# The low half of every expert's second down piece moves from VectorE to GpSimd

## The chip, the cores and the metric

The kernel runs on one core of one Trainium2 chip. The metric is device time in microseconds, from runs of the whole program. Engines are called as in the profile: PE (TensorE), PEld (its weight loads), DVE (VectorE), ACT (ScalarE), POOL (GpSimd), SP (SyncE, which here only issues DMAs).

## What is computed

The reference is a transformer block with two attention mixers and a mixture of experts, followed by a second block of two layers (dilated attention, then a gated linear recurrence, each beside attention over a memory). All tensors are float32, the sequence has 512 tokens of 1024 columns. The change is in the mixture of experts:

```
for e in range(N_EXPERTS):                                  # 32 experts, 8 groups of 4
    hid = silu(h @ w_gate[e]) * (h @ w_up[e])               # 1024 -> 256
    out = out + (hid @ w_down[e]) * combine[:, e:e + 1]     # 256 -> 1024
```

Each token has one group (the argmax of the group logits) and in it two experts with weights; `combine` is zero elsewhere.

## The kernel before

**Products in three passes.** Every weight matrix is streamed from HBM in pieces of up to 128 x 1024 float32 (512 KB) and split into a high half (ACT, a copy that rounds to the type fp32r, line 948, `hi_done`) and a low half (the piece minus its high half, line 1572 on DVE, `lo_done`). Activations are split in the same way. PE multiplies hi*hi, hi*lo and lo*hi (`PASSES`).

**Buffers.** A piece lies in one of RAW = 6 raw slots (`wraw`), its halves in one of SPL = 4 slots each (`whi`, `wlo`). SP loads the pieces in order; a load into a raw slot waits for `lo_done` of the piece that was there six pieces earlier (line 703). ACT makes the high half of piece p + 4 when PE has used piece p (`piece_used`, line 947). DVE makes a low half when the high half is there, and PE waits for the low half (line 2759). Six pieces of the experts (`HELD`, the first down pieces of experts 1, 5, 9, ...) are loaded ahead into memory of their own.

**The expert stage.** Tokens of a group are gathered into 128 rows (an indirect DMA of GpSimd into `x_row`), transposed and split. Expert n takes four gate/up pieces, each for two blocks of rows of both matrices; then the down product of expert n - 1 follows with its two down pieces, 0 and 1. So the order of the pieces is gu n 0, 1, 2, 3, dn n-1 0, 1, and so on, six for each expert. Each piece is six 512-column matmuls on PE.

PE's order for expert n: gate_up pieces 0 and 1; `hidden_t(n - 1)`, two transposes of the previous expert's hidden values; for the last expert of a group `columns`, four transposes of the next group's gathered rows; gate_up pieces 2 and 3; for the last expert of a group `columns` again; then `down(n - 1)`.

DVE's order for expert n (line 2009 on) follows one instruction behind another: feed of gu 0 (which makes the low half of the piece four further on, dn n-1 0), `hidden_lo(n - 1)` (line 2016), feed of gu 1 (the low half of dn n-1 1), for the last expert of a group `gathered` (four operations, line 1918), feed of gu 2, `hidden(n)` (line 2011), feed of gu 3, `gathered` again, feed of dn 0, for the first expert of a group `expert_sums` of the group before (line 2024, two operations, `y_done`), feed of dn 1. ACT has the same order with its own halves (`hidden_hi`, `silu`).

**GpSimd in the stage.** It issues the gathers and scatters. For group g it waits until the group's sums are made (`y_done`), scatters the rows to `x_moe` (line 860), waits for that (`y_out`), and gathers group g + 2 into the same rows (line 849). After the last group it waits until the last down piece has landed, and reloads x1 from `x_moe` (line 867).

**Low halves on GpSimd.** `lo_by_pool(p)` names pieces that DVE's `feed` leaves out. Before the change these are the `BESIDE_PICKS`, 16 pieces of the gate projections in the stage of the sparse attention's index, made by a loop at line 823.

Of the kernel before, what the change touches and what calls it, by code (L numbers as in the profile page):

```python
# [36 lines left out]
NGRP, EPG, FF = 8, 4, 256  # L37
# [70 lines left out]
def build(nc, A, out):  # L108
    ctx = ExitStack()
    with ctx:  # L110
# [5 lines left out]
        def S(name):  # L116
            if name not in sems:
                sems[name] = ctx.enter_context(nc.semaphore(name))
            return sems[name]
# [120 lines left out]
        NEXP = NGRP * EPG  # L240
        EXPERT_ORDER = [what for n in range(NEXP + 1)
                        for what in ([("gu", n, q) for q in range(4)] if n < NEXP else []) + ([("dn", n - 1, b) for b in range(2)] if n else [])]
        piece_of = {what: P_MOE + j for j, what in enumerate(EXPERT_ORDER)}
# [47 lines left out]

        BESIDE_PICKS = range(chunks[CH["ga0"]]["first"] + SPL, chunks[CH["gb0"]]["first"] + chunks[CH["gb0"]]["count"] + SPL)

        def lo_by_pool(p):

            return p in BESIDE_PICKS

        def slot_cols(p):
            return pieces[p][1] * pieces[p][2]
# [7 lines left out]
        def raw_slot(p):  # L307

            if p in HELD:
                return held[HELD.index(p)][:, 0:slot_cols(p)]  # L310
            return wraw[:, ring_at(p) % RAW, 0:slot_cols(p)]

        def raw_loaded(p):

            if p in HELD:
                return raw_held[HELD.index(p)], 96
            return raw_in[ring_at(p) % RAW], 96 * (ring_at(p) // RAW + 1)
# [412 lines left out]
        def wait_tp_read(eng, name, n):  # L730

            for par in range(2):
                last = max(u for u in range(TPU[name], TPU[name] + n) if u % 2 == par) if n > 1 or TPU[name] % 2 == par else None
                if last is not None:
                    eng.wait_ge(tp_free[par], last // 2 + 1)
# [20 lines left out]
        def _(pool):  # L756
# [63 lines left out]
                    r = pool.tensor_scalar(wi_s, idx1[:, :, 320:328], H8 ** -0.5, None, ALU.mult)  # L820
                r.then_inc(S("b_rot"), 1)

            for p in BESIDE_PICKS:
                pool.wait_ge(hi_done, p + 1)
                pool.tensor_tensor(w_slot(wlo, p, p % SPL), raw_slot(p), w_slot(whi, p, p % SPL).bitcast(F32),
                                   ALU.subtract).then_inc(lo_done[p % SPL], 1)

            wait_tp_read(pool, "ob", 4)
            pool.dma_start(x1, A["x"][0].rearrange("(t p) d -> p t d", p=P)).then_inc(S("res1"), 16)
# [18 lines left out]
            def gather(g):  # L848
                pool.indirect_dma_start(x_row[g % 2], None, x_all, bass.IndirectOffsetOnAxis(slot_from[:, g:g + 1], 0)
                                        ).then_inc(S(f"x_row_in{g % 2}"), 16)  # L850
# [4 lines left out]
            gather(1)  # L855
            pool.wait_ge(S("x_moe_in"), 32)
            pool.wait_ge(S("slot_to"), 1)
            for g in range(NGRP - 1):
                pool.wait_ge(S("y_done"), 2 * g + 2)
                pool.indirect_dma_start(x_moe, bass.IndirectOffsetOnAxis(slot_to[:, g:g + 1], 0), x_row[g % 2], None  # L860
                                        ).then_inc(S(f"y_out{g % 2}"), 16)
                pool.wait_ge(S(f"y_out{g % 2}"), 16 * (g // 2 + 1))
                if g + 2 < NGRP:
                    gather(g + 2)
            pool.wait_ge(*raw_loaded(piece_of["dn", NEXP - 1, 1]))
            for t in range(NT):
                pool.dma_start(x1[:, t, :], x_moe[t * P:t * P + P, :]).then_inc(S(f"x_back{t}"), 16)
# [70 lines left out]
        def _(act):  # L938
# [538 lines left out]
            for hh in range(2):  # L1477
# [25 lines left out]
                def decay(n):  # L1503
                    act.wait_ge(S("gl_e"), n + 1)
                    if n % 9 == 6:
                        (d1, d2), (_, second) = halves(kq[n % 5], 64), halves(G64[:, n // 9 % 4, :], 64)
                        act.activation(d2, second, ACT.Exp)
                        act.activation(d1, d1, ACT.Exp).then_inc(S("gl_x"), 1)
                        return
                    act.activation(kq[n % 5], kq[n % 5], ACT.Exp).then_inc(S("gl_x"), 1)  # L1510
# [47 lines left out]
        def _(dve):  # L1558
# [8 lines left out]
            def feed(p):  # L1567

                if p >= NP or lo_by_pool(p):
                    return  # L1570
                dve.wait_ge(hi_done, p + 1)
                dve.tensor_tensor(w_slot(wlo, p, p % SPL), raw_slot(p), w_slot(whi, p, p % SPL).bitcast(F32),  # L1572
                                  ALU.subtract).then_inc(lo_done[p % SPL], 1)
# [564 lines left out]
            for hd in range(9):  # L2138
                for i in range(12):
                    step, r = attention_step(i)  # L2140
                    if hd:
                        u = dil_unit(hd - 1, r)
                        U = u["U"]
                        c = U % 4
                        nm, mx = att_nm[:, c:c + 1], att_mx[:, 3 * c:3 * c + 3]
                        if step == "scores":
                            dve.wait_ge(att_s, U + 1)
                            at = 0
                            for g, (src, _, keys, mask, scale) in enumerate(u["s"]):
                                w = keys.shape[1]  # L2150
                                ins = dve.tensor_tensor_reduce(d_s[:, at:at + w], src[:, 0:w], mask, scale, LOW,
                                                               ALU.add, ALU.max, mx[:, g:g + 1])
                                at += w
                            link(ins)
                            link(dve.tensor_reduce(nm, mx, AX.X, ALU.max))
                            dve.tensor_scalar(nm, nm, -1.0, None, ALU.mult).then_inc(att_m, 1)  # L2156
                        elif step == "probs" and (i != 4 or hd == 8):
                            dil_probs(hd, r)
# [224 lines left out]
        def _(pe):  # L2383
# [519 lines left out]
            for hd in range(9):  # L2903
                for i in range(12):
                    step, r = attention_step(i)
                    if hd:
                        u = dil_unit(hd - 1, r)
                        U, name = u["U"], f"da{r}_{hd - 1}"
                        if step == "scores":
                            if r == 0:  # L2910
                                wait_tp_read(pe, f"dk_{hd - 1}", 3)
                            if U > AU["dil"]:
                                pe.wait_ge(att_done, outs(U))
                            for dst, q, k, _, _ in u["s"]:
                                mm = pe.matmul(dst[:, 0:k.shape[1]], q, k, start=True, stop=True)  # L2915
                            mm.then_inc(att_s, 1)
                        elif step == "probs":
                            pe.wait_ge(att_p, U + 1)
                            transposes(name, 0, [d_s[:, P * b:P * b + P] for b in range(4)])
                            transposes(name, 1, [d_s[:, P * b:P * b + P] for b in (4, 5)])  # L2920
                        else:
                            if r == 0:
                                read_all(f"vd{hd - 1}")
                            wait_tp_read(pe, name, 2)
                            for b, v in enumerate(u["v"]):
                                mm = pe.matmul(D_OUT, d_pt[:, P * b:P * b + P], v, start=b == 0, stop=b == 5)  # L2926
                            mm.then_inc(att_o, 1)
# [135 lines left out]
```

## Time and profile before

| | us |
|---|---|
| median of 3 runs | 2029.57 |
| lowest and highest run | 2026.38, 2033.82 |
| the profiled execution | 2037.6 |
| its span, first to last instruction | 2035.9 |
| PE busy in the span | 1951.7 (96%) |
| DVE busy | 1170.0 (57%) |
| ACT busy | 1025.1 (50%) |
| POOL busy | 316.8 (16%) |

The matmuls of the gate and up pieces (line 2783) run from 518.8 to 806 us of the span. In the tables of the profile a group of instructions is one line of the kernel with one engine and operation; "busy" is the time in which at least one of them ran, and the idle time behind it is what the engine waited just before. PE's ends are modelled, and matmuls overlap: one of 512 columns shows 0.39 us, but the next starts 0.23 us after it. The granted clock of the whole span is 0.992 of full speed.

### The profile page before, as it was taken

Reading aid. Unit: us, or ns where it says so; the run is one execution under the profiler, and the core shown is the slowest. Engines: PE = TensorE matmul, PEld = TensorE weight load, DVE = VectorE, ACT = ScalarE, POOL = GpSimd, SP = SyncE. Lnnn points to the kernel's source line nnn. Section 1 sums busy time; section 2 is a strip of 40 time slices with the busy share of each in tenths; the row PEclk is TensorE's granted clock in tenths of the full one; section 3 lists DMA queues with packets and bytes.
Section 4 is the critical chain, followed back from the end, with each engine's and each line's share of the span. In section 5 each row is a group of like instructions: output and inputs, shape, how many; then the busy total and the mean of one; then the engine's idle time right before and its main releaser. Section 6 shows DMA issues by size and latency. Waiting matters only on the chain.

```text
span 2035.9 us, 27851 instructions
## 1 busy us (share of the span) xinstructions
PE 1951.7 (96%) x10487; PEld 1683.2 (83%) x10487; DVE 1170.0 (57%) x2306; ACT 1025.1 (50%) x1689; POOL 316.8 (16%) x419
## 2 busy tenths in 40 slices
PE   7999999999999998999999999999999999998998
PEld 7977878777787776789999999999788778887887
DVE  3345388554899998753454445444443546746762
ACT  4654544344787777653544454445342555344341
POOL 1601232010010101201211121112010001401310
PEclk9999999999999999999999999999999999999999
DMA  4411221145899999523222222223243512122121
GB/s 146 144 42 42 73 73 63 42 136 217 286 363 370 352 367 349 174 57 86 63 72 74 69 67 70 71 70 94 77 150 95 175 42 73 43 73 57 58 104 42
DMA packets 178017, 255.58 MB, mean 126 GB/s; under 512 B 13565, under 2 KB 92234, under 8 KB 177882
## 3 DMA queue, kind: packets, MB, share of 16 engines
q1 hardware_dynamic: 168832, 221.33, 33.7%
q0 software_dynamic: 8784, 31.92, 4.2%
q8 instruction: 85, 1.39, 0.3%
q10 hardware_dynamic: 266, 0.52, 0.1%
q14 instruction: 50, 0.41, 0.1%
HBM read 239.57 MB, written 14.16 MB: 125 GB/s over the span
## 4 chain that ended last, share of the span: by engine, by line
PE 69%; DVE 15%; DMA 6%; ACT 5%; issue 2%; POOL 1%; SPq 0%; ACTq 0%; DVEq 0%
PE pb L2412 49%; DVE wlo L1572 6%; PE pb L2440 5%; DMA wraw<-w_down 3%; PE pb L3000 2%; ACT whi L948 2%; PE pb L2926 2%; PE pb L2496 2%; PE pb L2509 2%; PE pb L2915 2%; DMA wraw<-w_up 1%; PE pb L2783 1%; DMA wraw<-w_mem_kv 1%; DVE arena L2178 1%; PE pb L3023 1%
## 5 line engine op out<-in xcount | busy, mean ns | idle before, releaser
L1572 DVE TENSOR_TENSOR wlo<-wraw,whi 128x1024 fp32r<-128x1024 f32 (+4 forms) x430 | 489.2, 1151 | 533.4 <-ACT whi L948 532.1
L2412 PE MATMUL pb<-whi,AT_hi 128*128 128x512 f32 (+4 forms) x1864 | 725.5, 389 | 13.2 <-DVE arena L2178 5.4
L2412 PE MATMUL pb<-whi,AT_lo 128*128 128x512 f32 (+4 forms) x1864 | 677.4, 363 | 0.0
L2412 PE MATMUL pb<-wlo,AT_hi 128*128 128x512 f32 (+4 forms) x1864 | 675.7, 362 | 0.0
L948 ACT ACTIVATE whi<-wraw 128x1024 fp32r<-128x1024 f32 (+4 forms) x446 | 440.4, 994 | 393.8 <-PE pb L2412 327.0
L2412 PEld LDWEIGHTS pb<-whi,AT_hi 128*128 128x128 f32 x1864 | 352.6, 189 | 58.8 <-issue 19.8
L2412 PEld LDWEIGHTS pb<-wlo,AT_hi 128*128 128x128 f32 x1864 | 353.0, 189 | 39.5 <-issue 6.5
L2412 PEld LDWEIGHTS pb<-whi,AT_lo 128*128 128x128 f32 x1864 | 351.7, 189 | 39.8
L2440 PE MATMUL pb<-arena 128*128 128x128 f32 (+1 forms) x1116 | 169.7, 279 | 28.8 <-ACT arena L984 5.7
L2440 PEld LDWEIGHTS pb<-arena 128*128 128x128 f32 (+1 forms) x1116 | 137.5, 146 | 63.5 <-issue 11.3
L2783 PE MATMUL pb<-whi,AT_hi 128*128 128x512 f32 x256 | 105.3, 411 | 3.2 <-DVE wlo L1572 1.6
L2783 PE MATMUL pb<-whi,AT_lo 128*128 128x512 f32 x256 | 101.2, 395 | 0.0
L2783 PE MATMUL pb<-wlo,AT_hi 128*128 128x512 f32 x256 | 100.9, 394 | 0.0
L928 POOL TENSOR_TENSOR arena<-arena 128x256 f32<-128x256 f32 x72 | 64.3, 898 | 210.4 <-ACT arena L1510 200.8
L771 POOL TENSOR_TENSOR arena<-arena 128x64 f32<-128x64 f32 (+3 forms) x41 | 18.2, 444 | 479.6 <-DVE small L2193 333.3
L3000 PEld LDWEIGHTS pb<-arena 128*128 128x128 f32 x576 | 74.5, 191 | 9.6 <-issue 2.4
L3000 PE MATMUL pb<-arena 128*128 128x64 f32 (+2 forms) x576 | 76.0, 276 | 3.7 <-POOL arena L928 2.5
L1510 ACT ACTIVATE arena<-arena 128x512 f32<-128x512 f32 x64 | 39.5, 630 | 70.3 <-DVE arena L2295 54.6
L984 ACT ACTIVATE arena<-pb 128x512 f32<-128x512 f32 (+2 forms) x89 | 47.7, 571 | 37.4 <-PE pb L2440 37.4
L1040 ACT ACTIVATE arena<-pb,small 128x64 f32<-128x64 f32 x64 | 20.2, 316 | 87.2 <-PE pb L2509 87.2
L2783 PEld LDWEIGHTS pb<-whi,AT_hi 128*128 128x128 f32 x256 | 48.8, 191 | 17.9 <-DVE wlo L1572 7.5
L1401 ACT ACTIVATE arena<-arena,small 128x768 f32<-128x768 f32 x32 | 30.1, 940 | 63.5 <-DVE small L2156 63.5
(321 smaller groups left out, 2602.6 us busy)
## 6 DMA issues: line engine op xcount, KB each, us to landing
wraw<-w_in_a SPq DMA_DIRECT2D x288, 128.0 KB
wraw<-w_gate SPq DMA_DIRECT2D x128, 256.0 KB
wraw<-w_up SPq DMA_DIRECT2D x128, 256.0 KB
wraw<-w_down SPq DMA_DIRECT2D x58, 512.0 KB
wraw<-w_in_b SPq DMA_DIRECT2D x40, 512.0 KB
wraw<-w_in SPq DMA_DIRECT2D x28, 512.0 KB
wraw<-w_mem_kv SPq DMA_DIRECT2D x16, 512.0 KB
wraw<-w_in_a SPq DMA_DIRECT2D x16, 512.0 KB
```

Source lines behind the costliest of these rows:

```text
L928: pool.tensor_tensor(e2, q2, e2, ALU.mult).then_inc(S("gl_q"), 1)
L948: act.activation(w_slot(whi, p, p % SPL), raw_slot(p), ACT.Copy).then_inc(hi_done, 1)
L984: act.activation(dst, src, ACT.Copy, scale=scale).then_inc(tp_free[u % 2], 1)
L1572: dve.tensor_tensor(w_slot(wlo, p, p % SPL), raw_slot(p), w_slot(whi, p, p % SPL).bitcast(F32), ALU.subtract).then_inc(lo_done[p % SPL], 1)
L2412: mm = pe.matmul(ACC[bank][:, 0:n], a, b, start=kc == 0 and q == 0, stop=i == c["count"] - 1 and kk == per - 1 and q == 2)
L2440: tr = pe.transpose(TP[u % 2][0:b.shape[1], at:at + P], b, ident)
L2496: pe.matmul(SC[U % 2][:, 0:u["kw"]], u["q"], u["k"], start=True, stop=True).then_inc(att_s, 1)
L2509: mm = pe.matmul(TP[tu % 2][:, 0:u["dv"]], pt[:, P * b:P * b + P], u["v"][b], start=b == 0, stop=b == nb - 1)
L2783: mm = pe.matmul(ACC[n % 2].rearrange("p (w f) -> p w f", w=2), a, b, start=k == 0 and m == 0, stop=k == 7 and m == 2)
L2915: mm = pe.matmul(dst[:, 0:k.shape[1]], q, k, start=True, stop=True)
L2926: mm = pe.matmul(D_OUT, d_pt[:, P * b:P * b + P], v, start=b == 0, stop=b == 5)
L3000: mm = pe.matmul(dst, tile(k, s), rhs, start=True, stop=True)
```

## The change

GpSimd makes the low half of piece `("dn", n, 1)` for all 32 experts, and DVE leaves these pieces out. The helper `low_half` is the body of the old loop. The 32 calls are put into GpSimd's list between its waits, scatters and gathers: three before the loop over groups, four in each of its seven rounds, and one behind it. Nothing else is changed: the pieces, slots, semaphores and the orders of SP, ACT and PE are the same.

```
+        EXPERT_PICKS = [piece_of["dn", n, 1] for n in range(NEXP)]
+
         def lo_by_pool(p):
-            return p in BESIDE_PICKS
+            return p in BESIDE_PICKS or p in EXPERT_PICKS
...
+            def low_half(p):
                 pool.wait_ge(hi_done, p + 1)
                 pool.tensor_tensor(w_slot(wlo, p, p % SPL), raw_slot(p), w_slot(whi, p, p % SPL).bitcast(F32),
                                    ALU.subtract).then_inc(lo_done[p % SPL], 1)
+            for p in BESIDE_PICKS:
+                low_half(p)
...
             pool.wait_ge(S("slot_to"), 1)
+            for p in EXPERT_PICKS[0:3]:
+                low_half(p)
             for g in range(NGRP - 1):
+                low_half(EXPERT_PICKS[EPG * g + 3])
                 pool.wait_ge(S("y_done"), 2 * g + 2)
                 pool.indirect_dma_start(x_moe, ..., x_row[g % 2], None).then_inc(S(f"y_out{g % 2}"), 16)
+                low_half(EXPERT_PICKS[EPG * g + 4])
                 pool.wait_ge(S(f"y_out{g % 2}"), 16 * (g // 2 + 1))
                 if g + 2 < NGRP:
                     gather(g + 2)
+                low_half(EXPERT_PICKS[EPG * g + 5])
+                low_half(EXPERT_PICKS[EPG * g + 6])
+            low_half(EXPERT_PICKS[NEXP - 1])
             pool.wait_ge(*raw_loaded(piece_of["dn", NEXP - 1, 1]))
```

## Rows read from the trace of the kernel before

**Rows 1.** The page's 40 slices: DMA, busy share in tenths.

```profile
DMA  4411221145899999523222222223243512122121
```

**Rows 2.** Stretches: us, then engines' busy time (instructions), PE clock, DMA share, GB/s.

```profile
598.00:634.00 36.00, 35.13 (x162) 28.52 (x161) 33.80 (x43) 28.90 (x40) 3.85 (x2) 1.00 1.00 364
...
sum 254.12, PE 248.38 PEld 198.97 DVE 236.40 ACT 205.97 POOL 20.25; mean PE 35.48 PEld 28.42 DVE 33.77 ACT 29.42 POOL 2.89
```

**Rows 3.** Instructions of one line: ns min/median/max, first and last start in us.

```profile
L2011 DVE SCALAR_TENSOR_TENSOR arena<-pb,arena x32: 472/478/484, 528.7 to 807.9; 128x256 f32<-128x256 f32 x32
```

**Rows 4.** Waits of PE from 526 to 800 us: total, times, longest.

```profile
PE pb L2806 <- DVE AT_lo L2016: 2.2, 4, 1.1
PE pb L2783 <- DVE wlo L1572: 1.6, 6, 0.4
PE pb L2806 <- DVE wlo L1572: 1.5, 2, 0.8
PE pb L2440 <- DMA arena<-x_all,arena: 1.4, 2, 0.9
```

**Rows 5.** The instructions of GpSimd's line 825.

```profile
L825 POOL TENSOR_TENSOR wlo<-wraw,whi x16: 2357/2392/2413, 238.5 to 355.9; 128x1024 fp32r<-128x1024 f32 x16
```

**Rows 6.** Timeline of DVE, 590 to 603 us: start, duration, instruction.

```profile
590.09 3.48 DVE L1572 TENSOR_TENSOR wlo<-wraw,whi 128x1024 fp32r<-128x1024 f32 x3
...
598.76 1.28 DVE L2024 TENSOR_TENSOR arena<-pb,arena 128x512 f32<-128x512 f32 x2
...
602.23 0.41 DVE L2016 TENSOR_TENSOR AT_lo<-pb,AT_hi 128x256 fp32r<-128x256 f32 x1
602.56 2.35 DVE L1572 TENSOR_TENSOR wlo<-wraw,whi 128x1024 fp32r<-128x1024 f32 x2
```

**Rows 7.** Timeline of the stage of the index, 252 to 256 us.

```profile
252.50 0.62 DVE L1835 SCALAR_TENSOR_TENSOR arena<-arena,small 128x384 f32<-128x384 f32 x1 [0.73 <-DVE arena L1820]
...
253.44 2.39 POOL L825 TENSOR_TENSOR wlo<-wraw,whi 128x1024 fp32r<-128x1024 f32 x1 [5.42 <-ACT whi L948]
...
254.54 1.70 DVE L1835 SCALAR_TENSOR_TENSOR arena<-arena,small 128x384 f32<-128x384 f32 x1 [0.56 <-DVE arena L1820]
```

**Rows 8.** Timeline of the recurrence, 1731 to 1734 us.

```profile
1731.50 1.21 DVE L1572 TENSOR_TENSOR wlo<-wraw,whi 128x1024 fp32r<-128x1024 f32 x1
1732.04 1.38 POOL L928 TENSOR_TENSOR arena<-arena 128x256 f32<-128x256 f32 x1 [1.09 <-ACT arena L1510]
1732.63 1.07 DVE L2293 TENSOR_TENSOR arena<-arena 128x256 f32<-128x256 f32 x1
```

**Rows 9.** Timelines of GpSimd and DVE behind the expert stage.

```profile
847.89 2.86 POOL L890 TENSOR_SCALAR arena<-arena,small 128x1024 f32<-128x1024 f32 x1
...
848.12 0.75 DVE L1595 SCALAR_TENSOR_TENSOR AT_lo<-pb,arena,AT_hi 128x512 fp32r<-128x512 f32 x1 [2.23 <-ACT AT_hi L978]
```

**Rows 10.** Timeline of PE: first matmuls of D1, gate/up piece 3, D1.

```profile
595.62 0.39 PE L2806 MATMUL pb<-whi,AT_hi 128*128 128x512 f32 x1
...
601.30 0.42 PE L2783 MATMUL pb<-whi,AT_hi 128*128 128x512 f32 x1
...
604.21 0.39 PE L2806 MATMUL pb<-whi,AT_hi 128*128 128x512 f32 x1
```

**Rows 11.** GpSimd's scatters: one of the timeline, and all of line 860.

```profile
600.32 2.85 POOL L860 DMA_INDIRECT x_moe<-arena  x1 [26.24 <-DVE arena L2024]
...
L860 POOL DMA_INDIRECT x_moe<-arena x7: 1178/2852/2855, 564.9 to 784.7; - x7
```

**Rows 12.** Timeline of ACT: the high half of D1.

```profile
591.85 1.05 ACT L948 ACTIVATE whi<-wraw 128x1024 fp32r<-128x1024 f32 x1
```

**Rows 13.** The stage's end: PE's last down product; the reloads of x1.

```profile
813.22 0.47 PE L2806 MATMUL pb<-whi,AT_hi 128*128 128x512 f32 x1 [3.77 <-DVE AT_lo L2016]
...
L867 POOL DMA_DIRECT2D arena<-x_moe x4: 548/562/577, 807.3 to 809.0; - x4
...
DMA to landing us min/median/max: 7.3/9.4/12.0
```

More of the change, by code:

```diff
@@ L821, in _ @@
                 r.then_inc(S("b_rot"), 1)
-            for p in BESIDE_PICKS:
+            def low_half(p):
                 pool.wait_ge(hi_done, p + 1)
```

## The prediction

> **What bounds the kernel now.** The page's 40 slices come first: the change touches only the expert stage, and the row of DMA shares shows that stage as the block of nines in the tenth to sixteenth slices [rows 1]. The reader is to see that three quarters of the kernel have nothing to do with this change. Then the stage is cut into stretches of about 36 us, which is one group of four experts (31 experts pass from 528.7 to 807.9, 9.0 us each [rows 3]). In the stretch from 598 us PE is busy for 35.1 us, DVE for 33.8, and the DMA engines have a share of 1.00 at 364 GB/s [rows 2]. Three resources run side by side within a few per cent. Over seven stretches PE is busy for 248.4 of 254.1 us [rows 2], and its waits with a named releaser are short: 2.2 us for the low half of the hidden activations (L2016), 1.6 and 1.5 us for weight low halves (L1572), 1.4 us for a gather [rows 4]. PE is the bound; DVE, which makes all low halves, sets how much lead PE's operands have. So the question is not what the 32 subtractions cost DVE, but whether the lead survives when one in six goes to a slower engine.
>
> **The price of one piece.** GpSimd does this very operation in an earlier stage: 2.39 us for 128x1024, sixteen times, 2.36 to 2.41 us [rows 5]. DVE runs three of them in 3.48 us, one every 1.13 us when they are queued (the last one's end adds 0.09) [rows 6]. So 32 x 1.13 = 36 us leave DVE, and 32 x 2.39 = 76 us come to GpSimd, which is nearly idle in the stage. Were the engines independent, GpSimd's piece would only be ready 1.3 us later than DVE's.
>
> They are not independent. While GpSimd ran L825 from 253.44 to 255.83, a DVE operation with two SBUF inputs (L1835) took 1.70 us and ended 0.41 us after GpSimd; the same shape took 0.62 us just before [rows 7]. The other way round, GpSimd's operation at 1732.04 was held until DVE's low half ended at 1732.71 and ended 0.71 us after that, and DVE's next two-input operation ended 0.28 us after GpSimd's [rows 8]. So such operations exclude each other for their whole length, and GpSimd gets in between two of DVE's. An operation that reads PSUM and one SBUF tensor is not held: L1595, begun beside a GpSimd instruction, took 0.75 us [rows 9]; the hidden and gathered low halves are of that kind.
>
> The Trainium skill has this as a rule (SBUF — State Buffer, section "SBUF: two separate sides"): VectorE and GpSimd share one port pair as an exclusive lock, not as a split of bandwidth, and a DVE operation with two SBUF inputs contends for it with a GpSimd operation that reads SBUF. The rule speaks against this change; by it the piece costs DVE's list more than it frees, without it the lateness below would be about half. The trace agrees with it, by the 1.70 us against 0.62.
>
> For one group of four experts the time that DVE's list needs goes from 33.8 us [rows 2] by 4 x (2.39 - 1.13) = +5.0 to 38.8 us, beyond the 36.0 of the period [rows 3]. What can run beside GpSimd comes off: four hidden_lo at 0.33 us [rows 6] and one of the two runs of gathered, four PSUM-fed operations of half hidden_lo's columns, which I put at 1.1 us by that row. That leaves 36.4 to 38.8 us.
>
> **Walk through one group.** GpSimd's four pieces are laid into the times at hand. D1 is an expert's second down piece, and "late" is against PE's present start of it.
> - First (D1 before the gathered halves): DVE runs these beside GpSimd, and PE has its own transposes of the gathered rows before D1. Cost 0.
> - Second: DVE's three low halves run to 593.57 [rows 6], so GpSimd has 593.5 to 595.9; PE wants D1 at 595.62 [rows 10]. Late by 0.3 us. DVE resumes at 595.9 with low half, hidden (0.4), two low halves, the sums (L2024, 1.20) and one more low half: 595.9 + 4 x 1.13 + 0.4 + 1.2 = 602.0. PE wants that last one at 601.30 + 0.3 = 601.6 [rows 10]. Late by another 0.4 to 0.5. Together 0.8.
> - Third: the scatter (L860) is issued 0.3 us after the sums and occupies GpSimd for 2.85 us [rows 11], now from 601.2 to 604.05, since the sums end 0.9 later. Behind it in GpSimd's queue stands low_half: 604.1 to 606.5, against 604.21 + 0.8 = 605.0 [rows 10]. Late by 1.5 us, 2.3 in all. DVE's next low halves, held until 606.5, are then just in time.
> - Fourth: ACT makes the high half of D1 only after PE has used the piece four before and after hidden_hi: about 0.9 us, then 1.05 [rows 12], 2.39, and 0.2 for three hand-overs: 4.6 us. PE gets to D1 in three pieces of 1.4 us (601.30 to 604.21 is two [rows 10]) and 0.3 us of transposes: 4.5 us. Late by 0.1.
>
> That is 2.4 us per group, for the seven groups with sums and a scatter: 16.8 us. Two of the seven scatters are short (minimum 1.18 us, median 2.85 [rows 11]); there the third item is about 0.9 less: -1.8. PE's waits for a gather, 1.4 us [rows 4], are swallowed by the delay: -1.4. The first group has three D1 at 0.1 to 0.2: +0.5. Sum +14.1 us.
>
> **What else moves.** SP loads into a raw slot when its low half is made, and in order; a D1 slot is freed up to 2.8 us later (606.5 against 602.56 + 1.13 = 603.7 [rows 6]), and all later loads queue behind. PE is delayed too, by up to 2.3 of that; I take 0 and keep up to 1 us per group for the range. At the end of the stage the reloads of x1 (L867) went out at 807.3, when the last down piece had landed; now high half and low half stand before them, 1.05 + 2.39 = 3.5 us. They land 7.3 to 12.0 us after issue, so at 818.1 to 822.8; their reader comes after PE has ended the last down product, 813.22 + 4.5, and a first matmul behind it, 818 at the earliest [rows 13]. Between 0 and 4.8 us; I take 0, since the first tile is wanted first and was issued first. The waits on y_done and y_out (L859 to L864 of the kernel before) hold nothing that PE wants sooner: the low half in front of y_done is of an expert whose product the sums need anyway, and the next gather waits some 7 us more for the scatter to land, longer than the low half before it takes.
>
> Bounds of the whole: below, -5.3 us, if all of PE's waits for DVE in the stage vanish; above, 8 x 5.0 = +40 us, if nothing overlaps and PE feels all of it.
>
> **Rivals.**
> - *Hidden.* DVE idles for 36.0 - 33.8 = 2.2 us per group, and the delays are absorbed there: the loads catch up in them, and DMA, at 364 GB/s and a share of 1.00 [rows 2], goes on setting the period. Price: the low end of DVE's list, 36.4 against 36.0 us, 8 x 0.4 = +3.2 us. For it: the share of 1.00. Against it: PE has no idle time from which to give a delay back. The Trainium skill has a rule that points this way (same page, section "A bandwidth-pool intuition that's wrong"): HBM gives a core about 358 GB/s, by which the loads are at their ceiling. The trace has 364 in the stretch, so at or near it.
> - *Faster.* GpSimd's 2.39 us fall into DVE's idle time and beside its PSUM-fed operations, so DVE's list is shorter by 1.13 us where PE waits for it: PE's 5.3 us of waits for DVE [rows 4] go, and so do the 3.77 us that PE waits for L2016 at the end of the stage [rows 13]: -9.1 us. It decides only where D1 has at least 1.3 us of lead; at 604.21 DVE's low half had ended at 603.7, a lead of 0.5.
> - *Full price.* The high half of D1 is ready just when a two-input operation is next in DVE's list, nothing overlaps, and PE runs dry each time: +40 us. For it: two of the four steps above have a margin of 0.1 to 0.3 us. Against it: hidden_lo and gathered stand exactly at D1's place in DVE's list.
>
> **How the numbers follow.** The profiled execution took 2037.6 us (span 2035.9 and 1.7 around it); the median of the runs, 2029.6, is 8.0 lower, and I carry the difference over. Forecast +14.1: 2051.7 for a profiled execution, 2043.7 for the median; chance 0.52, its own range +6 to +24. Hidden: 2032.8, chance 0.25. Faster: 2020.5, chance 0.09. Full price: 2069.6, chance 0.14. About 0.5%, 10.1 us, is what a measurement can tell from no change. Of the forecast's 0.52, 0.44 lies above +10.1. So slower 0.44 + 0.14 = 0.58, same 0.08 + 0.25 = 0.33, faster 0.09. For 8 in 10 the range holds the forecast and Hidden, a third of Faster and half of Full price: 2025 to 2064.
>
> **What would show it.** GpSimd's group of low halves grows from 16 to 48 with a mean near 2.4 us or a little above; DVE's L1572 group has 32 fewer, and some that follow GpSimd take over 2 us instead of 1.22; PE waits at L2806 for GpSimd in most experts, longest (over 1 us) behind a scatter; a group takes 38 to 39 us; the DMA share falls to about 0.95. I would be wrong if groups still take 36 us (Hidden), if no DVE low half takes longer than 1.3 us (no exclusion), if PE's new waits are for gathers or loads (the slot release and the queue, which I took as 0), or if time moves outside 510 to 830 us.

## The result, and the profile after

The kernel after takes 2038.57 us (median of 15 runs, 2033.90 to 2042.37), the kernel before 2033.10 in the same comparison (15 runs, 2026.26 to 2039.22): a ratio of 1.0031, interval 1.0020 to 1.0041, so about 6.3 us slower (4.1 to 8.3). That is clear of the noise, inside the 0.5% that the prediction called no change, inside its range, and well short of the forecast's +14.1 us. The profiled execution after took 2038.1 us, the one shown before 2037.6: the second was 4.5 above its own median, the first at its own, so the two profiles differ by less than the runs do. What they can show is where the time within the stage is, not its sum.

The page first: DMA and GpSimd in 40 slices, and then, for the stretch of [rows 2], the same columns as there (us, busy time and instructions of each engine, PE clock, DMA share, GB/s), with the sum over the seven stretches.

```profile
POOL 1601232010233334201211121112010001401310
...
DMA  4511222146899999423222222223243512122131
```

```profile
598.00:634.00 36.00, 35.43 (x160) 27.68 (x159) 33.32 (x39) 28.66 (x40) 12.71 (x6) 1.00 0.99 359
...
sum 254.12, PE 247.82 PEld 195.64 DVE 234.29 ACT 204.67 POOL 86.80; mean PE 35.40 PEld 27.95 DVE 33.47 ACT 29.24 POOL 12.40
```

GpSimd's busy time in the seven stretches rises from 20.25 us [rows 2] to 86.80. DVE lost 28 operations of 1.2 us in them, some 34 us, and its busy time fell by only 2.1 (236.40 to 234.29): the rest is mostly time in which its other low halves were held. PE's busy time fell by 0.6 us. The DMA share of the stretch shown is 0.99 (1.00 before), where I had said 0.95.

The instructions of three lines: ns min/median/max, first and last start. GpSimd's low halves are 48 with a median of 2.40 us; DVE's longest low half is now 3.09 us (1.88 before); and the scatters, which occupied GpSimd for a median of 2.85 us [rows 11], take 1.72, all seven.

```profile
L1584 DVE TENSOR_TENSOR wlo<-wraw,whi x398: 547/1212/3087, 14.2 to 2010.6; 128x1024 fp32r<-128x1024 f32 x140, 128x768 fp32r<-128x768 f32 x48, 128x672 fp32r<-128x672 f32 x4, 128x384 fp32r<-128x384 f32 x3
...
L827 POOL TENSOR_TENSOR wlo<-wraw,whi x48: 2357/2402/3147, 238.6 to 807.6; 128x1024 fp32r<-128x1024 f32 x48
...
L868 POOL DMA_INDIRECT x_moe<-arena x7: 1712/1718/1721, 563.5 to 784.1; - x7
```

The waits of PE from 526 to 800 us (total, times, longest), against [rows 4]: those for a DVE low half fell from 3.1 us to 0.2, those for a gather (1.4) are gone, and the new one is for GpSimd, 3.4 us in ten waits. The four waits for L2016 (2.2 us) have become one of 2.6 us; what it is comes with the end of the stage, below. PE's weight loads wait for GpSimd too, so these rows are no full account.

```profile
PE pb L2818 <- POOL wlo L827: 3.4, 10, 0.9
PE pb L2818 <- DVE AT_lo L2028: 2.6, 1, 2.6
PE pb L2795 <- DVE wlo L1584: 0.2, 1, 0.2
```

One group in the timelines (start, duration, instruction, idle time before it and its releaser): GpSimd, then DVE, then three first matmuls of PE. It is the group that the prediction walked through, and PE is 1.3 us earlier in this profile.

```profile
591.87 2.40 POOL L827 TENSOR_TENSOR wlo<-wraw,whi 128x1024 fp32r<-128x1024 f32 x1 [7.15 <-ACT whi L960]
599.51 1.71 POOL L868 DMA_INDIRECT x_moe<-arena  x1 [5.23 <-DVE arena L2036]
601.25 2.50 POOL L827 TENSOR_TENSOR wlo<-wraw,whi 128x1024 fp32r<-128x1024 f32 x1
607.05 1.29 POOL L854 DMA_INDIRECT arena<-x_all,arena  x1 [3.30 <-DMA x_moe<-arena]
610.50 2.41 POOL L827 TENSOR_TENSOR wlo<-wraw,whi 128x1024 fp32r<-128x1024 f32 x1 [2.17 <-ACT whi L960]
```

```profile
588.30 3.48 DVE L1584 TENSOR_TENSOR wlo<-wraw,whi 128x1024 fp32r<-128x1024 f32 x3
591.70 0.41 DVE L2028 TENSOR_TENSOR AT_lo<-pb,AT_hi 128x256 fp32r<-128x256 f32 x1
593.16 2.20 DVE L1584 TENSOR_TENSOR wlo<-wraw,whi 128x1024 fp32r<-128x1024 f32 x1 [1.04 <-ACT whi L960]
...
601.75 3.08 DVE L1584 TENSOR_TENSOR wlo<-wraw,whi 128x1024 fp32r<-128x1024 f32 x1
```

```profile
594.33 0.50 PE L2818 MATMUL pb<-whi,AT_hi 128*128 128x512 f32 x1
...
600.41 0.50 PE L2795 MATMUL pb<-whi,AT_hi 128*128 128x512 f32 x1
...
603.80 0.50 PE L2818 MATMUL pb<-whi,AT_hi 128*128 128x512 f32 x1 [0.27 <-POOL wlo L827]
```

The exclusion is as forecast. GpSimd's piece of 591.87 ends at 594.27 and PE starts on it at 594.33; the DVE low half that stood ready from 593.16 took 2.20 us and ended 1.1 us after GpSimd. Behind the scatter GpSimd ran from 601.25 to 603.75, PE started at 603.80, and DVE's low half was held for 3.08 us. What is not as forecast is the size: from D1's first matmul at 594.33 to the next D1 at 603.80 are 9.47 us, against 8.59 [rows 10]. I had said 2.3 us late in all, 0.3 of it already at the first of the two, so 2.0 more between them; it is 0.9.

The matmuls of one line are too uniform for a view to group them by step, so I took each piece's first matmul from PE's timeline and the mean distance from one piece's start to the next, over groups 1 to 7 (the gather's row and the last one over groups 1 to 6). Groups and experts are counted from 0. D0 and D1 are the down pieces, gu0 to gu3 the gate/up pieces; the distance is named by the piece that it leads to. Here and below, a piece's e is the place in PE's order: D0 and D1 of e=1 stand behind the gate/up pieces of e=1 and belong to the expert before. The prediction's first step is then D1 of e=3, the second D1 of e=0 and gu3 of e=1, the third D1 of e=1, the fourth D1 of e=2. The two last columns are experiments (E6, E7 below). The steps left out differ by 0.12 us or less between before and after, and by 0.05 or less between E6 and E7.

```
us to the start of       before  after    E6     E7
D0 of e=0                 1.46   1.76    1.44   1.39
D1 of e=0                 1.38   1.43    1.37   1.43
gu0 of e=1 to 3 (mean)    1.37   1.47    1.37   1.46
gu3 of e=1 (past sums)    1.46   1.68    1.46   1.72
D0 of e=1                 1.57   1.49    1.38   1.52
D1 of e=1 (past scatter)  1.44   1.81    1.38   1.88
D0 of e=2                 1.70   1.39    1.36   1.36
gu2 of e=3 (gather)       2.34   1.97    1.99   1.98
four experts             36.35  36.40   34.64  35.88
```

### The profile page after: what moved, and what is told of

Its sections match the earlier page's. It is cut to its first block, busy times and chain, and to the rows that moved or that the text cites. A ratio compares the mean times of both kernels' runs of the same rounds, so it can differ in the third digit from the quotient of the medians.

```text
span 2036.5 us, 27851 instructions
## 1 busy us (share of the span) xinstructions
PE 1953.6 (96%) x10487; PEld 1682.8 (83%) x10487; DVE 1168.0 (57%) x2274; ACT 1026.4 (50%) x1689; POOL 391.9 (19%) x451
## 4 chain that ended last, share of the span: by engine, by line
PE 74%; DVE 12%; ACT 6%; DMA 4%; issue 3%; POOL 2%; SPq 0%; ACTq 0%; DVEq 0%; POOLq 0%
PE pb L2424 49%; PE pb L2452 5%; PE pb L2795 4%; DVE wlo L1584 4%; ACT whi L960 2%; PE pb L3012 2%; PE pb L2938 2%; PE pb L2818 2%; PE pb L2508 2%; PE pb L2521 2%; PE pb L2927 2%; DMA wraw<-w_up 1%; DMA wraw<-w_down 1%; DVE arena L2190 1%; DMA wraw<-w_mem_kv 1%
## 5 line engine op out<-in xcount | busy, mean ns | idle before, releaser
L1584 DVE TENSOR_TENSOR wlo<-wraw,whi 128x1024 fp32r<-128x1024 f32 (+4 forms) x398 | 482.6, 1226 | 530.8 <-ACT whi L960 529.8
L2424 PEld LDWEIGHTS pb<-whi,AT_hi 128*128 128x128 f32 x1864 | 352.6, 189 | 58.6 <-issue 19.8
L827 POOL TENSOR_TENSOR wlo<-wraw,whi 128x1024 fp32r<-128x1024 f32 x48 | 116.9, 2436 | 252.4 <-ACT whi L960 252.3
L2795 PE MATMUL pb<-whi,AT_hi 128*128 128x512 f32 x256 | 104.3, 408 | 1.5 <-DVE AT_lo L1930 0.7
L2818 PE MATMUL pb<-whi,AT_hi 128*128 128x512 f32 x128 | 54.8, 428 | 10.4 <-DVE AT_lo L2028 6.7
```

The lines of the kernel that those rows point to most:

```text
L2424: mm = pe.matmul(ACC[bank][:, 0:n], a, b, start=kc == 0 and q == 0, stop=i == c["count"] - 1 and kk == per - 1 and q == 2)
L2795: mm = pe.matmul(ACC[n % 2].rearrange("p (w f) -> p w f", w=2), a, b, start=k == 0 and m == 0, stop=k == 7 and m == 2)
L2818: mm = pe.matmul(ACC[2 + i], x, y, start=e == 0 and b == 0 and q == 0, stop=e == 3 and b == 1 and q == 2)
```

## Experiments

All kernels are compared with the kernel before on the same chip. The intervals are of 95%.

**E1: without the piece behind the scatter.** The third step was the forecast's largest (1.5 of 2.4 us per group). Here DVE keeps that low half.

```diff
+        KEPT = [EXPERT_PICKS[EPG * g + 4] for g in range(NGRP - 1)]
-            return p in BESIDE_PICKS or p in EXPERT_PICKS
+            return p in BESIDE_PICKS or p in EXPERT_PICKS and p not in KEPT
...
-                low_half(EXPERT_PICKS[EPG * g + 4])
```

> The changed kernel, but DVE keeps the D1 piece behind each of the seven scatters (experts 4, 8, ..., 28), so GpSimd makes 25 of the 32. In the changed kernel's trace the two steps from gate/up piece 2 to 3 and from D0 to D1 in these places are 0.2 and 0.4 us longer than before, the largest of its additions. Theory (the cost is PE waiting at D1 and just behind the sums): these 0.6 us go from seven groups, 4 us, so the ratio falls from 1.0031 to 1.001 (0.9995 to 1.002). Rival (the cost is the late release of raw slots, so that loads come later everywhere): seven of 32 slots come back, the ratio falls by a fifth only, to 1.0025.

Measured: 1.0024 (1.0010 to 1.0037). Its interval overlaps that of the change, so the runs don't tell them apart. In the profile the distance to D1 of e=1 goes back from 1.81 to 1.45 us, and that to D1 of e=2 rises from 1.67 to 2.06: the lateness moves to GpSimd's next piece. PE waits for the remaining GpSimd pieces 3.6 us in seven waits, as much as before the edit in ten (3.4). The step is real and worth 0.36 us, and taking it away gives nothing back. GpSimd's queue doesn't explain the shift in this run: in four of groups 1 to 6 the gather took 0.96 us, and the low half of D1 of e=2 behind it began 1.6 to 3.3 us later, when ACT released it.

```profile
608.25 0.96 POOL L855 DMA_INDIRECT arena<-x_all,arena  x1 [5.87 <-DMA x_moe<-arena]
611.12 2.40 POOL L828 TENSOR_TENSOR wlo<-wraw,whi 128x1024 fp32r<-128x1024 f32 x1 [1.92 <-ACT whi L960]
```

**E4: the scatter behind the low half.** The two change places in GpSimd's queue.

```diff
                 low_half(EXPERT_PICKS[EPG * g + 3])
+                low_half(EXPERT_PICKS[EPG * g + 4])
                 pool.wait_ge(S("y_done"), 2 * g + 2)
                 pool.indirect_dma_start(...)
-                low_half(EXPERT_PICKS[EPG * g + 4])
                 pool.wait_ge(S(f"y_out{g % 2}"), 16 * (g // 2 + 1))
```

> The changed kernel with the scatter of a group put behind the low half of the next D1 instead of ahead of it. Theory (exclusion between the two engines sets the lateness at D1, the scatter in the queue adds 0.5 us per group): D1 behind the scatter comes at its normal 1.4 to 1.5 us, 3 us are gained, but each scatter and gather goes out 4 to 5 us later, so PE's wait for gathered rows at the last expert of a group comes back if a gather had less than 5 us to spare (0.9 us was waited in one group before); ratio 1.001 to 1.004. Rival (GpSimd's queue costs nothing): 1.003 as the change, with no wait for gathers.

Measured: 1.0146 (1.0119 to 1.0172), 40.82 us per group. Slower, but by another way than I wrote: PE never waits for a gather. Its waits from 526 to 840 us, and GpSimd's timeline through one boundary:

```profile
PE pb L2818 <- POOL wlo L827: 22.0, 16, 3.6
PE pb L2818 <- DVE AT_lo L2028: 4.0, 1, 4.0
```

```profile
606.47 3.20 POOL L827 TENSOR_TENSOR wlo<-wraw,whi 128x1024 fp32r<-128x1024 f32 x1 [6.28 <-ACT whi L960]
609.82 1.80 POOL L869 DMA_INDIRECT x_moe<-arena  x1 [0.16 <-issue]
618.40 0.96 POOL L854 DMA_INDIRECT arena<-x_all,arena  x1 [6.77 <-DMA x_moe<-arena]
619.38 2.60 POOL L827 TENSOR_TENSOR wlo<-wraw,whi 128x1024 fp32r<-128x1024 f32 x1
```

The scatter is issued 3.35 us behind the start of the low half, where in the change it went 1.74 us ahead of it. GpSimd then stands 6.77 us at its wait for the landing (y_out), and the low half of D1 of e=2, in the queue behind that wait, starts only at 619.38. In the change the same wait ended at 607.05, and ACT released that low half only at 610.50, so the wait cost nothing. By the ratios the other order is better by 0.0115, 23 us. Not all of that is waiting. Behind its wait of 3.62 us PE runs at the lower of its two clock levels (1.2 GHz, not 2.4) for a while: its matmuls there start 0.43 us apart instead of 0.23, and the granted clock of the stretch from 598 us is 0.95 (1.00 in the change).

```profile
622.03 0.73 PE L2818 MATMUL pb<-whi,AT_hi 128*128 128x512 f32 x1 [3.62 <-POOL wlo L827]
...
598.00:634.00 36.00, 32.04 (x137) 25.12 (x136) 28.61 (x31) 25.30 (x36) 13.16 (x6) 0.95 0.91 318
```

The two pieces behind D1 of e=2 take 2.26 and 2.18 us (groups 1 to 6), 1.48 and 1.37 in the change: 1.6 of the 4.4 us by which a group is longer.

**E5: the other down piece.** GpSimd makes D0 instead of D1: behind a scatter PE wants it one piece, 1.4 us, sooner.

```diff
-        EXPERT_PICKS = [piece_of["dn", n, 1] for n in range(NEXP)]
+        EXPERT_PICKS = [piece_of["dn", n, 0] for n in range(NEXP)]
```

> The changed kernel, but with the first down piece D0 of every expert on GpSimd instead of D1. DVE's next entries behind D0 are hidden_lo (0.33 us, reads PSUM) and the low half of D1 (two SBUF inputs). PE needs D0 1.4 us earlier after ACT's high half than... the same three pieces after the piece four before it; but hidden_hi does not stand ahead of it in ACT's list, so it has 0.9 us more lead. Theory (lead decides): D0 comes in time, D1's low half on DVE is then held up to 2 us and comes 0 to 0.5 us late; ratio 1.001 to 1.003. If lead did not matter but only exclusive time (rival): the same as the change, 1.003.

Measured: 1.0075 (1.0054 to 1.0096), 38.01 us per group. GpSimd's and PE's timelines behind one scatter:

```profile
602.41 1.71 POOL L868 DMA_INDIRECT x_moe<-arena  x1 [6.36 <-DVE arena L2036]
604.15 2.38 POOL L827 TENSOR_TENSOR wlo<-wraw,whi 128x1024 fp32r<-128x1024 f32 x1
```

```profile
606.58 0.50 PE L2818 MATMUL pb<-whi,AT_hi 128*128 128x512 f32 x1 [1.60 <-POOL wlo L827]
```

PE waits for the end of the same two instructions as in the change, now for 1.60 us instead of 0.27: the distance to this piece is 3.27 us. So GpSimd's queue behind the scatter does hold PE, and the piece that stands between D0 and D1 covers most of it in the change. The third step's mechanism stands.

**E8: half a piece each.** DVE makes the left 512 columns of each D1, GpSimd the right 512.

```diff
+                pool.wait_ge(S("left_half"), EXPERT_PICKS.index(p) + 1)
+                pool.tensor_tensor(wlo[:, p % SPL, 512:1024], raw_slot(p)[:, 512:1024], ...
...
+                if p in EXPERT_PICKS:
+                    dve.wait_ge(hi_done, p + 1)
+                    dve.tensor_tensor(wlo[:, p % SPL, 0:512], ...).then_inc(S("left_half"), 1)
+                    return
```

> The changed kernel, but D1 is split: DVE makes the low half of columns 0 to 511, GpSimd after it that of columns 512 to 1023, and PE waits for the second part only before its second three matmuls. GpSimd's part should take 1.2 us instead of 2.4, and D1 is whole about 1.8 us after its high half instead of 2.5. Theory: PE's waits at D1 (3.4 us in ten places of the changed kernel's trace) vanish, while the gains from the overlap of gathered and hidden_lo with GpSimd shrink; ratio 1.000 (0.998 to 1.002). Rival (slot release and DMA decide, not D1): the slot is freed 0.7 us earlier only, 1.002.

Measured: 1.0040 (1.0022 to 1.0058), no better than the change, where I had hoped for 1.000. GpSimd's and DVE's timelines:

```profile
606.14 2.19 POOL L865 TENSOR_TENSOR wlo<-wraw,whi 128x512 fp32r<-128x512 f32 x1 [1.29 <-DVE wlo L1588]
```

```profile
605.38 0.68 DVE L1588 TENSOR_TENSOR wlo<-wraw,whi 128x512 fp32r<-128x512 f32 x1
605.97 1.21 DVE L1594 TENSOR_TENSOR wlo<-wraw,whi 128x1024 fp32r<-128x1024 f32 x1
```

GpSimd's half is released by DVE's half, and by then DVE has begun its next low half: GpSimd is held by it until 607.18 and ends 1.15 us later. The half that takes 1.27 to 1.30 us alone took 2.19.

**E2 and E3: the subtraction beside a DVE list that keeps all its pieces.** Both start from the kernel before. At the places where the change has a low half, GpSimd subtracts 128x1024 numbers in memory that nothing uses (E2), or fills as long a stretch of it (E3, 2.37 us, no SBUF input).

```diff
+            def beside(n):
+                pool.wait_ge(hi_done, piece_of["dn", n, 1] + 1)
+                link(pool.tensor_tensor(spare[:, 0:1024], spare[:, 1024:2048], spare[:, 2048:3072], ALU.subtract))
```

```diff
+                link(pool.memset(spare[:, 0:2700], 0.0))
```

> The kernel before, DVE making all low halves, and in addition GpSimd runs a 128x1024 subtraction of unused memory (two SBUF inputs, as L825) at each place where the change has a low_half, released by the same hi_done. Nobody waits for its result. It prices the exclusion alone. Theory: DVE's list for four experts is 33.8 us plus 4 x 2.39 less up to 2.4 beside PSUM-fed operations, 41 us against 36: +5 us per group, +35 to +42 us, ratio 1.017 to 1.021. Rival (the two engines do not hold each other in this stage, or share): ratio 1.000 to 1.003.

> The same as the kernel before with a GpSimd instruction at each of the 32 places, but a memset of 128x2700 of unused memory, about 2.4 us long, which reads no SBUF. Theory (only a GpSimd operation that reads SBUF excludes DVE's two-input operations): no DVE low half beyond 1.3 us, ratio 1.000 to 1.002. Rival (any GpSimd operation takes the port pair, writes too): as the subtraction, 1.017 to 1.021.

Measured: E2 1.0228 (1.0197 to 1.0259), 41.38 us per group, 5.0 more than before; E3 1.0017 (1.0002 to 1.0031), 36.29 per group. GpSimd's instruction and DVE's low halves from 526 to 840 us (times, then busy us and mean ns, idle time before and its releaser), in E2 and in E3:

```profile
L1585 DVE TENSOR_TENSOR wlo<-wraw,whi 128x1024 fp32r<-128x1024 f32 x175 | 263.3, 1543 | 3.6 <-ACT whi L961 3.5
...
L862 POOL TENSOR_TENSOR arena<-arena 128x1024 f32<-128x1024 f32 x30 | 80.0, 2665 | 153.2 <-ACT whi L961 153.0
```

```profile
L1585 DVE TENSOR_TENSOR wlo<-wraw,whi 128x1024 fp32r<-128x1024 f32 x188 | 224.1, 1219 | 24.1 <-ACT whi L961 22.5
L862 POOL MEMSET arena<- 128x2700 f32 x32 | 75.7, 2366 | 137.1 <-ACT whi L961 137.0
```

With nearly the same busy time of GpSimd, DVE's mean low half is 1543 ns beside subtractions and 1219 beside fills, and its idle time in front of them falls from 24.1 us to 3.6. The exclusion needs a GpSimd operation that reads SBUF. The Trainium skill says so (SBUF — State Buffer, section "SBUF: two separate sides"): a DVE operation with two SBUF inputs takes the shared ports from GpSimd only against one that reads SBUF. By that rule E2 is held and E3 is not, as measured. (The lower end of E3's interval lies just above 1, which leaves room for a small cost of its own; its groups in the profile don't show one.) In E2 DVE's list is the bound (busy for 36.0 of 36.0 us from 598): 33.8 us and four times 2.39 are 43.4, of which 2.0 overlap.

**E6 and E7: before and after with fewer loads.** The forecast had PE as the bound, its rival the loads. Here the loads of w_up are left out of both kernels (the gate/up products use what the slot holds; all other work is the same).

```diff
-                pieces.append(([... for i, w in enumerate((gate_rows, up_rows))], 1, PIECE))
+                pieces.append(([... for i, w in enumerate((gate_rows,))], 1, PIECE))
```

> The kernel before without the loads of w_up (the up half of each gate/up piece is left as it lies in the slot): the expert stage loads a third less. It shows what DMA costs the kernel before. Theory (PE is the bound and DMA close behind): PE's 1 to 4 us of waits that go back to late loads vanish, ratio 0.994 to 1.000, with the DMA share near 0.7.

> The changed kernel without the loads of w_up, to be compared with e6. Theory (the change's cost is lateness at D1 and behind the sums, not loads): e7 over e6 is the same +5 to +8 us as the change over the kernel before, or a little less. Rival (the late release of raw slots with DMA at its ceiling carries the cost): e7 over e6 is 0 to +2 us.

Measured: E6 0.9953 (0.9938 to 0.9968), E7 0.9999 (0.9984 to 1.0014). The stretch from 598 us in E6 and in E7:

```profile
598.00:634.00 36.00, 36.00 (x167) 29.77 (x166) 35.39 (x45) 30.75 (x41) 7.45 (x3) 1.00 0.80 258
```

```profile
598.00:634.00 36.00, 35.64 (x162) 28.38 (x161) 33.65 (x39) 29.78 (x41) 12.39 (x6) 1.00 0.77 249
```

Two things follow. A group needs 34.64 us on PE, not 36.0: with all loads the kernel before took 36.35 and so lost 1.7 us per group to them, though PE read as 98% busy and its named waits were few. The loads show at ACT, which reads each piece first: from 526 to 840 us it waited 26.8 us for w_up and 15.0 for w_down in the kernel before, 26.4 and 4.8 in the change, and in E6 only 4.4, for w_down. And with the loads out of the way the same change costs more: 1.24 us per group, 10.4 us from expert 1 (counted from 0) to D1 of the last in the profiles, 10.6 by the medians (2032.09 - 2021.48) and 9.4 by the ratios. The price of the change is therefore not made by late slot releases or by the load queue; it is PE's lateness, and the loads hide about 4 of 10 us.

**E9 and E10: only the piece beside the gathered halves.** The first step was taken as free. Here only those seven D1 (each group's third expert's, the D1 of e=3 of the table) go to GpSimd, with all loads (E9) and with w_up's left out (E10).

```diff
-        EXPERT_PICKS = [piece_of["dn", n, 1] for n in range(NEXP)]
+        EXPERT_PICKS = [piece_of["dn", EPG * g + 2, 1] for g in range(NGRP - 1)]
```

> GpSimd makes only seven low halves, those of D1 of experts 2, 6, ..., 26, beside which DVE runs gathered and hidden_lo (1.4 us fed from PSUM); DVE keeps the other 25. In the changed kernel's trace this step cost PE nothing, and DVE came out of it 0.5 us further ahead. Theory (the lead at D1 decides): no addition anywhere, DVE's list is shorter just ahead of the second gathered and the sums, PE's waits for L2016 (2.2 us before) shrink; ratio 0.998 to 1.0005. Rival (any hand-over to GpSimd costs through the lock or the slots, a share of the change's cost): 7/32 of 0.3%, 1.0007, or more.

> The same seven low halves on GpSimd, without the loads of w_up, to be compared with e6_light_before (0.9953, 34.64 us per group). Theory: 34.6 us per group, ratio 0.995, no wait of PE for GpSimd. Rival: 34.7 to 34.9 us, a share of the 1.24 us that all four pieces cost in e7.

Measured: E9 0.9994 (0.9980 to 1.0008), E10 0.9962 (0.9949 to 0.9975) against E6's 0.9953 (0.9938 to 0.9968); 34.68 us per group against 34.64. This piece costs nothing that can be measured, and it brings nothing.

**E11: E1 with fewer loads,** to see whether the lateness that came back in E1 is the loads' or GpSimd's. The edits are those of E1 and E6; one line of them:

```diff
-                low_half(EXPERT_PICKS[EPG * g + 4])
```

> e1 (DVE keeps D1 behind the scatter) without the loads of w_up, to be compared with e7_light_after (0.9999, 35.88 us per group) and e6. There the third step is not covered by loads. Theory (lateness at D1 is additive where nothing else binds): the 0.5 us of D1 and 0.14 of D0 behind the scatter go, 35.2 to 35.4 us per group, ratio 0.9972 to 0.998, and what e1 did not gain had been given back to the loads. Rival (the lateness only moves to the next GpSimd piece): 35.8, ratio 0.9995.

Measured: 1.0013 (1.0002 to 1.0024), 35.95 us per group, against E7's 0.9999 and 35.88. The theory (a gain) failed and the rival held: D1 of e=1 goes from 1.88 to 1.45 us, D1 of e=2 from 1.36 to 1.89. GpSimd's, DVE's and PE's timelines there:

```profile
607.31 5.10 POOL L855 DMA_INDIRECT arena<-x_all,arena  x1 [3.53 <-DMA x_moe<-arena]
612.43 2.40 POOL L828 TENSOR_TENSOR wlo<-wraw,whi 128x1024 fp32r<-128x1024 f32 x1
```

```profile
606.96 3.48 DVE L1584 TENSOR_TENSOR wlo<-wraw,whi 128x1024 fp32r<-128x1024 f32 x3
610.37 1.21 DVE L1584 TENSOR_TENSOR wlo<-arena,whi 128x1024 fp32r<-128x1024 f32 x1
611.50 0.41 DVE L2028 TENSOR_TENSOR AT_lo<-pb,AT_hi 128x256 fp32r<-128x256 f32 x1
612.96 2.97 DVE L1584 TENSOR_TENSOR wlo<-wraw,whi 128x1024 fp32r<-128x1024 f32 x1 [1.04 <-ACT whi L960]
```

```profile
614.89 0.50 PE L2818 MATMUL pb<-whi,AT_hi 128*128 128x512 f32 x1 [0.41 <-POOL wlo L828]
```

The gather's instruction began inside DVE's run of four two-input low halves and ended only 0.8 us after that run, at 612.41, and GpSimd's low half of D1 of e=2 stood behind it. In E7 the gather of the same group came at 606.56, in front of such a run, and took 0.97 us. So an instruction of GpSimd that only issues a DMA can take 4 us longer too, and it holds the low halves behind it. This is the cause in E11; in E1 the same shift came mostly with short gathers, behind ACT's high half, so the two share the result and not the reason.

## Why the prediction was off in size

- **Exclusion, and that PE comes late at D1 and behind the sums: right.** The held DVE low halves (2.20, 3.08 us), PE starting within 0.1 us of GpSimd's end, E2's 5.0 us per group and E3's groups of 36.29 us, no longer than before, show it. The sum of DVE's list, 4 x 2.39 less overlap, is a real bound where no pieces leave it (E2).
- **The sign for *Hidden*, that groups still take 36 us: it came.** They take 36.40 us, 36.35 before, where I had said 38 to 39.
- **First step, 0: right.** E9 and E10.
- **Second step, 0.3 at D1 and 0.4 to 0.5 behind the sums: mis-sized.** E7 against E6 gives 0.06 and 0.26. Before, DVE's three low halves ended 2.05 us ahead of PE's D1 [rows 6, 10], too little for GpSimd's 2.40; after, 588.30 + 3.48 = 591.78 is 2.55 us ahead of 594.33, and it was ACT's high half that released GpSimd. The 2.05 was no property of the list. Over groups 1 to 6 this lead is 2.18 us before, 2.44 in the change, and with fewer loads 2.61 without any move (E6) and 2.45 with it (E7). Nor is it won by the first step: that alone leaves it at 2.20 (E9), and at 2.45 with fewer loads (E10). So the kernel before had a lead cut short while it lost time to the loads, and I priced the step from it; what lifts it in the change stays open. DVE also idled 1.04 us for ACT before 593.16, so not all of GpSimd's 2.40 us fell on it.
- **Third step, 1.5: the term that failed most.** E7 against E6 gives 0.50 at D1 and 0.14 at D0 in front of it; in the change itself 0.37 at D1, and D0 comes 0.08 sooner. I took the scatter at 2.85 us from [rows 11]. It took 1.72 in all seven, so low_half began 1.74 us after the scatter, not 2.9. That is the 1.0 us by which the term was too large. In the group shown the scatter even began earlier than the prediction's time (599.51 against 601.2, of which 1.3 are the profiles' shift). The price rests on a duration that isn't fixed: in E6, which has no low half on GpSimd, five of the seven scatters took 1.72 us as well.
- **Fourth step, 0.1: small, as written.** D1 of e=2 comes 0.12 us later in the change (1.67 against 1.55) and no later in E7 (1.36 against 1.40). The first piece behind D1, gu0 of e=1 to 3, is some 0.1 us later each time, a term that I had not written, worth 0.3.
- **Sum.** 2.4 us per group were written. Without the load bound 1.24 are measured (E7 less E6), about 10 us for the whole. That the result lies just inside the forecast's own range, +6 to +24, is in part luck: the sum was about twice too large per group, the loads hid about 4 us that it didn't take off, and the end of the stage added some 2 that it didn't have.
- **The gather waits, -1.4: they went**, and a little more: the distance to the piece that waits for it fell from 2.34 to 1.97, 2.2 us over six groups.
- **"PE is the bound", and the delays added to a period of 36.0: wrong.** E6 shows PE's floor at 34.64. I had excluded *Hidden* because PE "has no idle time from which to give a delay back". It had: 1.7 us per group are lost to loads in waits too short or unnamed to show in the table of waits, and PE's busy time, with modelled ends, read 35.1 of 36. *Hidden* said that loads go on setting the period and absorb the delay; they absorb about 4 of 10 us. So the result lies between the two cases, as their mechanisms both hold.
- **Slot release and queue, 0: right** in that the cost is larger without the load bound (E7 less E6), not smaller.
- **x1 reloads, 0: small.** They went out at 810.3 instead of 807.3 [rows 13] and landed 6.2 to 10.7 us later; their reader started at 821.22 us against 820.54.
- **The end of the stage, a term that I had not written.** From gate/up 0 of expert 28 to D1 of expert 31 PE took 46.06 us against 43.72. Of the 2.3 us, 2.16 are one step, D0 of e=0 in group 7 (4.14 us against 1.98). At the start of that group DVE runs four operations on 128x128 numbers in SBUF, each with one tensor and a column of scalars as inputs; before and after:

```profile
775.92 0.87 DVE L2033 TENSOR_SCALAR arena<-arena 128x128 f32<-128x128 f32 x4
...
773.99 3.00 DVE L2045 TENSOR_SCALAR arena<-arena 128x128 f32<-128x128 f32 x4
774.28 2.43 POOL L827 TENSOR_TENSOR wlo<-wraw,whi 128x1024 fp32r<-128x1024 f32 x1 [6.12 <-ACT whi L960]
778.61 0.47 PE L2818 MATMUL pb<-whi,AT_hi 128*128 128x512 f32 x1 [2.62 <-DVE AT_lo L2028]
```

GpSimd's low half began 0.3 us after their start and they ended 0.3 us after its end, 2.1 us late; `hidden_lo`, which follows in DVE's list, came late by as much, and PE waited 2.62 us for it. So the exclusion isn't confined to operations with two SBUF inputs, as the prediction had it. In the four runs in which a GpSimd subtraction overlaps these four operations (the change, E1, E2, E5) they take 3.0 to 3.1 us; in the nine in which none does, 0.86 or 0.87. D0 and D1 of the last expert add 1.4 us, and other steps of the stretch are 1.2 us shorter. In E7 the four operations are free (0.87 us) and the stretch is still longer than in E6, 43.33 us against 41.01, 2.0 of it at the last expert's two down pieces.

Open: the split of 6.3 us between the seven boundaries and the end (in the profiles 3.3 us from expert 1 to the last, 2.3 of them at the end, where the start of the stage varies by 4 us from profile to profile), and whether E1 differs from the change.

## What to carry to other kernels

Two engines' operations that exclude each other make one list: before moving a piece, add up both engines' times in it, and then look for a place where the first engine runs something exempt; only there is the piece free, and there it may bring nothing. Look at what else the first engine runs beside it, once per kernel too: four operations of 0.2 us each cost PE 2.2 us here. Read a duration of a DMA-issuing instruction as a result of what ran beside it, not as a constant, and look at every wait behind it in the same queue: E4's reordering of two instructions cost 23 us more than the change. When three resources read 94 to 100%, take work off one of them in both kernels; it says which is the bound, and what the change costs where that one is not.

## What the runs showed of the hardware

GpSimd's instruction that issues an indirect DMA has no fixed length. Its ns (min, median, max) in the kernel after and in E11, for the gathers of the stage:

```profile
L854 POOL DMA_INDIRECT arena<-x_all,arena x8: 973/1107/1898, 507.5 to 751.9; - x8
```

```profile
L855 POOL DMA_INDIRECT arena<-x_all,arena x8: 1056/5000/5189, 509.7 to 751.0; - x8
```

The same gather takes 1.0 us or 5.1. In E11 six of the eight take 4.6 to 5.2 us and each is issued into a run of four of DVE's low halves with two SBUF inputs, as in E6, where the six take 3.9 to 5.2; in E7, with GpSimd's low half in front, they take 0.97 to 1.02. The Trainium skill says that a tensor_tensor of DVE with both inputs in SBUF contends with GpSimd's reads, and infers that it leaves the writing of DMA descriptors alone (SBUF — State Buffer, section "Who interferes with whom"). A gather's list of indices lies in SBUF, so the first half fits; by the second half DVE's run should not have held it; where it did, the measurement decides. But such a run alone isn't enough: in E5 a gather began 0.33 us into a run of three and was done after 1.72 us, 1.4 us before the run ended.

```profile
609.41 1.72 POOL L854 DMA_INDIRECT arena<-x_all,arena  x1 [2.88 <-DMA x_moe<-arena]
...
609.08 3.48 DVE L1584 TENSOR_TENSOR wlo<-wraw,whi 128x1024 fp32r<-128x1024 f32 x3
```

So that DVE's run is the cause is read from the timelines of E6, E7 and E11; no run changed it alone, and what else it takes, and why a scatter takes 1.2, 1.7 or 2.85 us, stays open.
